# One decode-and-prompt layer on one core: squares of the row tiles earlier, key weights of the compress stage loaded earlier, bias sums with the weights as the moving operand

## What is computed

```
def mix_prompt(h, lp):
    u, v, q, kv_c, kv_s, kv_w, gate = split_proj(h, lp['w_in'], lp['gate_b'])
    o_a, v_rows = gmlp_mix(u, v, ...)
    k_c, v_c, ... = nsa_context(kv_c, kv_s, lp)
...
def compress(k, pe, w1, b1, w2):
    n = (T - CMP_LEN) // CMP_STRIDE + 1
    idx = jnp.arange(n)[:, None] * CMP_STRIDE + jnp.arange(CMP_LEN)[None, :]
    blk = k[:, idx] + pe[None, None, :, None, :]
    blk = jnp.transpose(blk, (0, 1, 3, 2, 4)).reshape(B, n, G, CMP_LEN * Dh)
    return jax.nn.gelu(blk @ w1 + b1) @ w2
```

## Time and profile before

| | us |
|---|---|
| median of 3 runs | 1769.87 |
| lowest and highest run | 1766.8, 1775.65 |
| profiled execution, its own time | 1766.52 |
| its span in the profile | 1764.7 |
| PE busy (9867 matmul records) | 1628.5 (92%) |
| PEld busy | 1405.4 (80%) |
| DVE busy | 808.1 (46%) |
| ACT busy | 498.1 (28%) |
| POOL busy | 492.0 (28%) |

### The profile page before, as it was taken

The page is one execution under the profiler, slowest core; times in us unless marked ns, Lnnn a source line. Parts: engine busy times, 40 slices in busy tenths (PEclk is TensorE's granted clock), DMA queues, the critical chain, the costliest instruction groups (busy, mean ns, idle before and its releaser), DMA issues.

```text
span 1764.7 us, 26695 instructions
## 1 busy us (share of the span) xinstructions
PE 1628.5 (92%) x9867; PEld 1405.4 (80%) x9867; DVE 808.1 (46%) x1503; ACT 498.1 (28%) x1038; POOL 492.0 (28%) x491
## 2 busy tenths in 40 slices
PE   6899999788777999999899999999999999999995
PEld 5799998677346667766677989998999899988994
DVE  3393311042225789998345153335333533354337
ACT  4222322022103666777233211111111111111112
POOL 2272422261303444454212131113111311131112
PEclk9899999699886999999999999999999999999998
DMA  5032122433702000000501112111211121112102
GB/s 197 25 117 82 51 87 53 84 96 96 225 1 69 4 7 4 4 1 1 179 0 37 36 36 72 36 36 36 71 36 36 36 70 37 36 36 60 47 12 96
DMA packets 97896, 99.04 MB, mean 56 GB/s; under 512 B 6776, under 2 KB 83161, under 8 KB 97721
## 3 DMA queue, kind: packets, MB, share of 16 engines
q1 hardware_dynamic: 79706, 77.61, 14.6%
q0 software_dynamic: 4880, 12.96, 2.5%
q10 hardware_dynamic: 13232, 7.41, 1.5%
HBM read 90.81 MB, written 11.34 MB: 58 GB/s over the span
## 4 chain that ended last, share of the span: by engine, by line
PE 80%; DVE 8%; issue 3%; ACT 3%; DMA 3%; POOL 2%; ACTq 1%; POOLq 0%; SPq 0%; DVEq 0%
PE bankpair L2234 9%; PE bankpair L2236 9%; PE bankpair L2235 9%; PE bankpair L2261 5%; PE bankpair L2262 5%; PE bankpair L2263 5%; PE bankpair L365 3%; PE bankpair L369 3%; PE bankpair L366 3%; PE bankpair L998 3%; PE bankpair L1774 3%; PE bankpair L1854 2%; PE bankpair L1743 2%; PE bankpair L1855 2%; PE bankpair L1856 2%
## 5 line engine op out<-in xcount | busy, mean ns | idle before, releaser
L2234 PE MATMUL bankpair<-h2T_high,w_high 128*128 128x344 f32 x1056 | 337.6, 320 | 0.0
L2236 PE MATMUL bankpair<-h2T_high,w_low 128*128 128x344 f32 x1056 | 337.1, 319 | 0.0
L2235 PE MATMUL bankpair<-h2T_low,w_high 128*128 128x344 f32 x1056 | 337.1, 319 | 0.0
L2285 POOL TENSOR_TENSOR w_low<-work,w_high 128x1024 fp32r<-128x1024 f32 x44 | 105.3, 2415 | 566.5 <-ACT w_high L2280 566.4
L2364 DVE TENSOR_TENSOR x_all<-x_all,bankpair 128x512 f32<-128x512 f32 (+1 forms) x396 | 251.6, 683 | 1.6
L2350 DVE TENSOR_TENSOR kT_space<-kT_space,bankpair 128x344 f32<-128x344 f32 x66 | 33.9, 513 | 451.4 <-ACT kT_space L2298 451.4
L2298 ACT ACTIVATE kT_space<-bankpair 128x344 f32<-128x344 f32 x66 | 30.3, 459 | 624.1 <-PE bankpair L2236 624.1
L2234 PEld LDWEIGHTS bankpair<-h2T_high,w_high 128*128 128x128 f32 x1056 | 198.6, 188 | 2.9
L2235 PEld LDWEIGHTS bankpair<-h2T_low,w_high 128*128 128x128 f32 x1056 | 198.1, 188 | 0.8
L2236 PEld LDWEIGHTS bankpair<-h2T_high,w_low 128*128 128x128 f32 x1056 | 198.4, 188 | 0.0
L365 PE MATMUL bankpair<-win_high,h_high 128*128 128x256 f32 (+2 forms) x648 | 188.8, 291 | 1.3 <-ACT h_high L534 0.5
(11 more groups left out here) (310 smaller groups left out, 2823.5 us busy)
## 6 DMA issues: line engine op xcount, KB each, us to landing
work<-in_w_gate SPq DMA_DIRECT2D x22, 512.0 KB, 5.1
work<-in_w_up SPq DMA_DIRECT2D x22, 512.0 KB, 6.3
work<-in_w_down SPq DMA_DIRECT2D x22, 512.0 KB, 3.8
x_all<-in_x_prompt SPq DMA_DIRECT2D x15, 512.0 KB, 11.0
work<-in_w_in SPq DMA_DIRECT2D x7, 1024.0 KB, 5.1
work<-in_cache_kv_cmp SPq DMA_DIRECT2D x32, 128.0 KB, 2.6
work<-in_cache_kv_cmp POOLq DMA_DIRECT2D x32, 128.0 KB, 3.2
work<-in_cache_kv_slc POOLq DMA_DIRECT2D x32, 128.0 KB, 3.8
```

Source lines behind the costliest of these rows:

```text
L2234: pe.matmul(out, wh, high, start=(k == 0), stop=False)
L2235: pe.matmul(out, wh, low, start=False, stop=False)
L2236: ins = pe.matmul(out, wl, high, start=False, stop=(k == KD - 1))
L2285: pool.tensor_tensor(w_low[s][x], w_raw[s][x], w_high[s][x].bitcast(F32), ALU.subtract).then_inc(gu_low, 1)
```

## The change

It does five things. `square_x` runs one place earlier in ScalarE's queue (t + 4 instead of t + 3), and the low part of chunk 1 stands behind all `inv_x` on POOL. The first piece of chunk 0's weights is rounded and subtracted ahead of the second square. The key weights are loaded when chunk 7 is done instead of chunk 8, into another place (`w1[0]` at 4096); the sorted rows lie in `regC`, where they need only wait for the mixer's transposes. In the bias sums `peT` is the stationary operand (one column) and `w1` moves (128 columns); the result is a row, which VectorE copies and TensorE turns into a column; the sum of the values now stands between the two halves of the first `hidden`. And because the places moved, `stream_kv` of sequence 0 waits for the last transposes, and `t_win` is loaded together with `t_slc`, with one wait for both.

```
         square_x(act, 0)
+        round_first(act, 0)
         square_x(act, 1)
-        for piece in range(len(FIRST)):
+        for piece in range(1, len(FIRST)):
             round_first(act, piece)
         take_hT(act, 0)
+        square_x(act, 2)
         take_hT(act, 1)
-        square_x(act, 2)
+        square_x(act, 3)
         for t in range(XT):
             if t + 2 < XT:
                 take_hT(act, t + 2)
-            if t + 3 < XT:
-                square_x(act, t + 3)
+            if t + 4 < XT:
+                square_x(act, t + 4)
             take_z(act, 0, t)
...
         inv_x(0)
+        low_first(0)
         inv_x(1)
-        for piece in range(len(FIRST)):
+        for piece in range(1, len(FIRST)):
             low_first(piece)
         for t in range(2, XT):
             inv_x(t)
-            if t == 6:
-                low_w_in(pool, 1)
+        low_w_in(pool, 1)
...
-    w1 = [at(0, [16, P]), at(2048, [16, P])]
+    w1 = [at(4096, [16, P]), at(0, [16, P])]
-    sorted_rows = at(4096, [4, 4, P])
+    sorted_rows = at(0, [4, 4, P], regC)
+    bias_row = at(9216, [2, P])
...
         sp.wait_ge(z_ready, XT * (NC - 1))
+        load_w_cmp(sp, 0)
         load_raw(sp, 1, 0, raw_ready)
         sp.wait_ge(z_ready, XT * NC)
-        load_w_cmp(sp)
+        load_w_cmp(sp, 1)
...
         elif a < 2:
-            eng.wait_ge(z_ready, XT * (NC - 1))
+            eng.wait_ge(oaT_ready, XT)
...
-        def sum_bias():
-            pe.wait_ge(w_cmp_ready, 160)
-            pe.wait_ge(oaT_ready, XT)
+        def turn_bias():
+            pe.wait_ge(w_cmp_ready, 128)
             for kv in range(2):
                 ins = pe.transpose(pb(4)[:, 16 * kv:16 * kv + 16], pe_raw[0:16, kv, :], ident[0:16, 0:16])
             ins.then_inc(pe_turned, 1)
+
+        def sum_bias(kv):
             pe.wait_ge(pe_taken, 1)
-            for kv in range(2):
-                for r in range(16):
-                    ins = pe.matmul(pb(5)[:, kv:kv + 1], w1[kv][:, r, :], peT[:, kv, r:r + 1], start=(r == 0), stop=(r == 15))
+            if kv:
+                pe.wait_ge(wv_tslc_ready, 32)
+            for r in range(16):
+                ins = pe.matmul(pb(6 + kv)[0:1, 0:P], peT[:, kv, r:r + 1], w1[kv][:, r, :], start=(r == 0), stop=(r == 15))
             ins.then_inc(bias_summed, 1)
+
+        def turn_sum(kv):
+            pe.wait_ge(pe_taken, kv + 2)
+            pe.transpose(pb(6 + kv)[:, P:P + 1], bias_row[0:1, kv, :], ident[0:1, 0:1]).then_inc(bias_summed, 1)
...
             for kv in range(2):
+                if w == 0:
+                    sum_bias(kv)
                 for r in range(16):
...
                 ins.then_inc(hid_summed, 1)
+                if w == 0:
+                    turn_sum(kv)
...
                 turn_pairs(s)
+                if s == 0:
+                    turn_bias()
             if w >= 1:
                 compressed(w - 1)
-            else:
-                sum_bias()
             hidden(w)
...
-                    act.wait_ge(bias_ready, 1)
+                    act.wait_ge(bias_ready, kv + 1)
...
-            dve.wait_ge(bias_summed, 1)
-            dve.tensor_tensor(hid_bias, pb(5)[:, 0:2], b1, ALU.add).then_inc(bias_ready, 1)
+            for kv in range(2):
+                dve.wait_ge(bias_summed, 2 * kv + 1)
+                dve.tensor_copy(bias_row[0:1, kv, :], pb(6 + kv)[0:1, 0:P]).then_inc(pe_taken, 1)
+                dve.wait_ge(bias_summed, 2 * kv + 2)
+                dve.tensor_tensor(hid_bias[:, kv:kv + 1], pb(6 + kv)[:, P:P + 1], b1[:, kv:kv + 1], ALU.add).then_inc(bias_ready, 1)
...
         if s == 0:
-            eng.wait_ge(hid_summed, 2 * (NW - 1))
-        if s == 1:
             eng.wait_ge(pairs_turned, 4 * NS)
...
                 sp.wait_ge(hid_summed, 2 * NW)
-                sp.dma_start(t_slc[0:64], C["t_slc"]).then_inc(t_slc_ready, 16)
+                sp.dma_start(t_slc[0:64], C["t_slc"][:, 0:PAST]).then_inc(wv_tslc_ready, 16)
+                sp.dma_start(t_win[0:64], C["t_win"][:, 0:512]).then_inc(wv_tslc_ready, 16)
...
+        dve.wait_ge(wv_tslc_ready, 64)
         link(dve.tensor_tensor(s_win[0:64, 0:512], pb(0)[0:64, :], t_win[0:64, 0:512], ALU.add))
         dve.tensor_reduce(st_s[0:64, 1:2], s_win[0:64, :], AX, ALU.max, negate=True).then_inc(max_s, 1)
-        dve.wait_ge(t_slc_ready, 16)
```

More of the change, by code:

```diff
@@ L868, in build_program @@
     NS = NB + 1
-    w_cmp_ready = sem("w_cmp_ready")
+    w_cmp_ready, wv_tslc_ready = sem("w_cmp_ready"), sem("wv_tslc_ready")
     raw_ready = [sem("raw_ready0"), sem("raw_ready1")]
@@ L885, in load_cmp_small, with load_w_cmp @@
             sp.dma_start(pe_raw[0:16, kv, :], A[npe][0].rearrange("(r t) d -> r (t d)", t=2)).then_inc(w_cmp_ready, 16)
-    def load_w_cmp(sp):
-        for kv, (n1, _, _, _) in enumerate(W_CMP):
-            for b in range(2):
-                sp.dma_start(w1[kv][:, 8 * b:8 * b + 8, :], A[n1][0, D * b:D * b + D].rearrange("(r p) h -> p r h", p=P))\
-                  .then_inc(w_cmp_ready, 16)
+    def load_w_cmp(sp, kv):
+        name = W_CMP[kv][0]
+        for b in range(2):
+            sp.dma_start(w1[kv][:, 8 * b:8 * b + 8, :], A[name][0, D * b:D * b + D].rearrange("(r p) h -> p r h", p=P))\
+              .then_inc(w_cmp_ready if kv == 0 else wv_tslc_ready, 16)
     def stage2_sync(sp):
@@ L988, in hidden @@
             pe.wait_ge(pairs_odd, 2 * (2 * w + ns))
-            if w == 0:
-                pe.wait_ge(bias_ready, 1)
-            else:
+            if w:
                 pe.wait_ge(hid_ready, 2 * w)
             for kv in range(2):
+                if w == 0:
+                    sum_bias(kv)
                 for r in range(16):
@@ L1128, in build_program @@
     pT_win = at(2818, [4, 64])
-    t_win = at(KVS, [513], regC)
+    t_win = at(4096, [512])
     q_bd = at(2052, [NB, NH], regC)
@@ L1134, in build_program @@
     oT_s = at(2708, [64], regC)
-    t_slc = at(3074, [PAST + 1])
+    t_slc = at(3072, [PAST])
     t_cmp = at(13312, [CMP_N])
@@ L1154, in build_program @@
     pnT = at(13174, [2, 64])
-    table_ready, t_slc_ready = sem("table_ready"), sem("t_slc_ready")
+    table_ready = sem("table_ready")
     kv_in = [sem("kv_in0"), sem("kv_in1")]
@@ L1202, in load_tables @@
     def load_tables(sp):
-        for dst, name, n in ((t_win, "t_win", 64), (t_cmp, "t_cmp", 64), (imp_add_s, "imp_add_s", 64),
+        for dst, name, n in ((t_cmp, "t_cmp", 64), (imp_add_s, "imp_add_s", 64),
                              (same_group, "same_group", 64), (seq_rows, "seq_rows", 8), (rows_seq, "rows_seq", 64),
@@ L1220, in stage3_tensor @@
     def stage3_tensor(pe):
-        pe.wait_ge(table_ready, 112)
+        pe.wait_ge(table_ready, 96)
         pe.wait_ge(q_sorted, 1)
@@ L1359, in stage3_vector @@
         dve.tensor_copy(knT, pb(0)[:, 96:112].rearrange("p (b s) -> p b s", b=2))
-        dve.wait_ge(table_ready, 112)
+        dve.wait_ge(table_ready, 96)
         link(dve.tensor_tensor(gate_rows[0:64, :], pb(1)[0:64, 0:24], head_pick[0:64, :], ALU.mult))
@@ L1704, in stage4_sync @@
         sp.wait_ge(kv_split, 2)
-        sp.wait_ge(table_ready, 112)
+        sp.wait_ge(table_ready, 96)
         sp.dma_start(mask_cmp, C["mask_cmp"]).then_inc(table_ready, 16)
@@ L1809, in stage4_tensor @@
                     pe.wait_ge(kc_ready, NW)
-                    pe.wait_ge(table_ready, 144)
+                    pe.wait_ge(table_ready, 128)
                     pe.wait_ge(kaug_ready, 32)
@@ L2040, in select_blocks @@
                 dve.wait_ge(pc_normed, i + 1)
-                dve.wait_ge(table_ready, 144)
+                dve.wait_ge(table_ready, 128)
             if part >= 2:
```

## The result

The changed kernel takes **1727.5 us** (median of four runs, 1725.1 to 1730.0) against 1769.0 for the kernel before in the same comparison (1766.8 to 1775.7): a ratio of 0.976, 95% interval 0.9735 to 0.9789. The forecast was 1732. The profiled execution took 1727.93, its span is 1726.1; before they were 1766.52 and 1764.7.

A forecast was written before the change was run, and what follows sets the result against it. TensorE bounds nearly everywhere, with gains in the first chunk and compress stage: 15.5 + 21.1 - 0.5 = 36.1 us, giving 1730.4 from the profiled run or 1733.8 from the median; forecast 1732, range 1725 to 1745.

The forecast's parts named there:

- the hole: First chunk: TensorE's 7.88 us idle before tile 7, behind GpSimd's low part of chunk 1, would go.
- the lower end of the range: 1725 us: 1730.7 from the fastest run, less the mixer's 3.1 wait and 0.5 each from copies and page loads.
- Squares two places ahead: First chunk: scale and turn no longer wait for the square; rounds fall from 5.48 to 4.24 us, gaining 4.9 us.
- Low part behind the scales: First chunk: the 7.88 us hole and the slow clock behind it go, gaining 10.5 us.
- rival 3: First chunk: GpSimd's low part of chunk 1 blocks VectorE's scale of tile 8, up to 4.4 us lost, 1736; chance 0.08.
- First piece before the second square: First chunk: 0.6 us of rounding moves into ScalarE's wait for x tile 1; counted as nothing.
- The mixer's wait: Behind the first chunk: TensorE's 3.1 us wait on VectorE's chain moves along and stays.
- Compress stage: From 306.56 us, 23.8 us would stand where 44.9 stood, gaining 21.1 us.
- rival 1: Compress stage: clock is down when the first bias sum begins and returns in it; +3.2 us, 1735; chance 0.10.
- Rival 2: Compress stage: one-column products don't hold or raise the clock; sums and hidden halves slow, +10.5 us, 1742; chance 0.12.
- rival 5: Compress stage: a new TensorE wait for value weights inside the hidden product replaces the old; chance 0.05, 0.03 slower.
- Streams: Before the first key turn: stream_kv(0) waits 2.7 us longer, later loads share the DMA; 0.5 us lost, bounds 0 and 2.7.

The follow-up runs named there:

- the second comparison: The changed kernel run again unaltered, beside two further variants, against the kernel before on the same chip: 1730.3 us, ratio 0.980.
- experiment 2: The kernel before with only the low part of chunk 1 moved behind all scales of x: 1766.8 us.
- experiment 3: The kernel before with the low part behind all scales, GpSimd also waiting until VectorE has scaled the last tile: 1767.6 us in one run.
- experiment 4: The changed kernel with ScalarE's rounding of chunk 1 one tile earlier: 1733.2 us.
- experiment 5: The kernel before with all edits of stage 1 (squares, low part, first weight piece), compress stage as before: 1750.4 us, ratio 0.990.
- experiment 7: The changed kernel with the key weights loaded behind the last chunk again, ahead of the value weights: 1746.9 us.
- experiment 8: The changed kernel with the bias sums turned back to weights stationary and one column moving: 1736.8 us.
- experiment 9: The changed kernel with the t_win load issued on SP behind the slc pages of sequence 5: 1726.4 us in one run.

## Why the prediction was right

The total was 4.5 us from the forecast. The path was the one forecast: the rounds lost their wait, the hole went, the sums ran at full clock, no long wait took the place of the old one. Sizes were off, and two terms that were added are not independent. In spans 38.6 us were gained for 36.1 forecast: 2.6 more in stage 1, 1.1 more in the compress stage, 0.9 less by the streams and 0.3 less behind. The other 2 us come from the starting point, taken between one execution and the median, and the runs scatter as much: the second comparison gave 1730.3. The terms named for the lower end of the range add up to 1730.7 - 3.1 - 1.0 = 1726.6, not 1725; the median lies above both.

- **Squares two places ahead.** The mis-sized term: a round was put at 4.24 us and took 3.70. I had subtracted only the idle time from 5.48. But the wait had cost more than its idle: before, the first product stood 43.46 - 42.28 = 1.18 us behind the start of a turn, after, 38.82 - 38.03 = 0.79; and the turn now begins 0.16 inside the modelled end of the last product (37.91 + 0.28 against 38.03). That is 1.23 + 0.39 + 0.16 = 1.78 a round. The four rounds gave 4 x 1.78 = 7.1, not 4.9; the squares alone gave 8.6.
- **Low part behind the scales.** 10.5 was forecast for it, and from the turn of tile 6 to the products of tile 7 the change won (61.90 - 42.28) - (42.40 - 34.33) = 11.5. The size was near, but it isn't this edit's own: alone it gave nothing (experiment 2), and with the block out of the way 7.5 over the same stretch (experiment 3, (61.90 - 42.28) - (54.68 - 42.58)); the rest is two more rounds at 3.70 us, which the squares bring. The forecast counted both as terms to be added; they are not, since the early squares are also what brings the last scale 1.22 us ahead of GpSimd. "By my count the scale ends just as GpSimd starts" was the right thing to look at: by the trace, it ended 0.05 us after (39.65 and 39.60). What counts is which of the two begins first. Nothing in the edits was meant to secure that: ScalarE's rounding holds GpSimd back, and one tile earlier it no longer does (experiment 4). The 0.08 given to rival 3 was small for what stood on it, 6.2 us between experiments 2 and 3 and 4.7 in experiment 4.
- **First piece before the second square, and the mixer.** Costed at nothing, and no run tests it alone. The 0.8 us gained ahead of the turn of tile 2 can't be put down to it: that turn starts between 18.95 and 20.52 in the eight profiles with the edit and between 20.36 and 20.66 in the five without. The mixer's wait stayed at 3.2 us. Of the 19.5 us gained at tile 7's products (7.1 and 11.5 as above, and this 0.8), 1.4 was given back before the end of stage 1, which the forecast didn't have. It is the clock behind the mixer's wait, which fell earlier in this profile; experiment 5, with the same edits, gives nothing back there.
- **Compress stage.** 21.1 forecast, 22.2 measured. Sums 7.4 and 7.30; hidden product 13.9 and 14.14; copies 1.0 and 0.92; the new wait for the sort 0.7 and 0.69. Of the 1.1 more, 0.4 is the two small transposes, which now run inside the wait for the sort of sequence 1 (285.47), and 0.6 is the stretch from the next transposes to the next hidden product (6.65 us before, 6.04 after). The row of decode products was the right neighbour: 0.114 us a record.
- **Clock (rivals 1 and 2).** 1.00 from 283 to 304, over both sums. The sums with 128 columns moving neither began nor ran at the lower level. Experiment 7 shows the case of rival 1: the first sum begins at 0.50, the clock comes back in it, and it costs 1.7 us, not 3.2. Rival 2's worry was right for the form that was taken out: with one column moving, the same place costs 7.8 us (experiment 8), of the 10.5 it was priced at. The rule of the Trainium skill (TensorE: Matmul & The Clock Gate, Part 4: PE-mode transpose) isn't borne out here: TensorE did little but transposes from 283 to 289 and kept 1.00.
- **Key and value weights (rival 5).** No wait on either. Without the early load, 10.4 us of waiting and 3.4 of slow clock come back (experiment 7).
- **Streams.** 0.5 was put against the change; 1.4 was measured up to the first key turn, inside the bounds of 0 and 2.7. 0.8 of it is the releasing load, which landed in 5.37 us for 4.57; its cause isn't the table (experiment 9). The other 0.6 is the clock: behind the wait of 5.60 us, which the kernel before has too, the third hidden product begins 27.56 us after the second, for 26.94 before, and the granted clock is still 0.50 from 343 to 345, the end of that stretch, where before it was back at 0.96 (384 to 386).

## What to carry to other kernels

When an edit lets a long GpSimd pass run beside VectorE, look up in the timeline which of the two begins first, to the tenth of a microsecond: one order cost some 5 us here, the other nothing, and an edit elsewhere can turn it round. Two edits that meet at such a point are tried together and apart, since their gains don't add. And where a product can be written with either operand moving, try both and read the granted clock of the work behind it too: a wait, or one form of a small product, is paid there a second time.

## What the runs showed of the hardware that was not expected

- A wait of TensorE of 1.2 us per round cost 1.78: 0.39 more between turn and first product, and 0.16 of overlap with the last product.
- Behind the same wait of 3.15 us the granted clock was still 1.00 in one profile and 0.50 at once in another, and 1.4 us up to the end of the stage hung on it.
- In the first sum with one column moving TensorE was busy without a gap and its granted clock was 0.61; in the same sum with the operands exchanged it was 1.00.
- VectorE's small TENSOR_SCALAR on 128 x 4 numbers, 0.17 us alone, took 3.05 beside GpSimd's low part, ending with it, while a TENSOR_REDUCE on 128 x 256 ran its 0.40 us there undisturbed (54.64, experiment 3).
